# Expert stage of a two-block model: gathered expert rows replaced by both expert tables streamed once

## What is computed

```python
q = (hb @ w_q).reshape(T, 8, 2, 128)
s = einsum('thpc,hpkc->thpk', q, sub_keys)            # 8 heads, 2 halves, 128 keys each
top_s, top_i = top_k(s, 16)
cand_s = top_s[:, :, 0, :, None] + top_s[:, :, 1, None, :]      # 16 x 16 sums
fin_s, fin_pos = top_k(cand_s.reshape(T, 8, 256), 16)
idx = take_along_axis(top_i0 * 128 + top_i1, fin_pos)  # 16 of 16384 experts, per head
gates = softmax(fin_s)
act = gelu(einsum('thkd,td->thk', expert_u[idx], hb))
out = einsum('thk,thkd->td', gates * act, expert_v[idx])
```

## Time and profile before

| what | us |
|---|---|
| three runs | 1610.01, 1617.12, 1620.13 |
| median | 1617.12 |
| span of the profiled execution, first to last instruction | 1608.7 |
| median less that span | 8.4 |

### The profile page before, as it was taken

One profiled execution on the slowest core, in us unless ns is written; L12 is line 12 of the kernel. 1 busy time (PEld: TensorE's weight loads), 2 busy tenths in 40 slices (PEclk: granted clock), 3 DMA queues, 4 the chain that ended last, 5 costly groups with the idle time before them and its releaser, 6 DMA issues.

```text
span 1608.7 us, 22053 instructions
## 1 busy us (share of the span) xinstructions
PE 1490.8 (93%) x7680; PEld 1122.0 (70%) x7682; DVE 944.0 (59%) x2391; ACT 412.9 (26%) x1006; POOL 597.0 (37%) x525
## 2 busy tenths in 40 slices
PE   8999899989899877777799999999999999999997
PEld 7999845554445323223247788999998888899997
DVE  5652587666766776676457734555553145555554
ACT  2110223222222232222115521121123145311112
POOL 4860234334344444443333105555520000455551
PEclk9999999999999999999999999999999999999999
DMA  8464699999999999999994227444424220544431
GB/s 334 157 232 166 256 427 427 426 411 427 427 423 426 425 427 427 427 427 390 426 399 163 76 100 283 166 163 170 139 107 156 105 79 1 213 168 157 157 130 39
DMA packets 63383, 420.63 MB, mean 261 GB/s; under 512 B 7340, under 2 KB 7788, under 8 KB 16812
## 3 DMA queue, kind: packets, MB, share of 16 engines
q0 software_dynamic: 38560, 277.19, 41.5%
q1 hardware_dynamic: 24736, 142.35, 24.8%
HBM read 417.28 MB, written 3.45 MB: 262 GB/s over the span
## 4 chain that ended last, share of the span: by engine, by line
PE 66%; DMA 20%; issue 5%; DVE 4%; POOL 3%; ACT 2%; SPq 0%; POOLq 0%; DVEq 0%
DMA arena<-uv_dram,arena 18%; PE bank L2309 15%; PE wide L2349 9%; PE wide L2110 9%; PE bank L1841 6%; PE bank L1867 4%; PE bank L1960 2%; PE bank L1931 2%; POOL arena L503 2%; PE bank L2476 2%; PE bank L1921 2%; PE bank L2277 2%; PE bank L1818 2%; ACT arena L663 1%; PE bank L2132 1%
## 5 line engine op out<-in xcount | busy, mean ns | idle before, releaser
L2110 PE MATMUL wide<-arena 128*128 128x512 f32 x1024 | 473.0, 609 | 95.7 <-ACT arena L663 95.5
L2110 PEld LDWEIGHTS wide<-arena 128*128 128x128 f32 x1024 | 189.7, 193 | 356.5 <-issue 194.2
L1388 DVE CUSTOM_DVE_ANT_0 arena<-arena,wide 128x1024 f32<-128x1024 f32 x256 | 312.5, 1221 | 191.4 <-DMA arena<-uv_dram,arena 186.5
L503 POOL DMA_INDIRECT arena<-uv_dram,arena x256 | 259.4, 1013 | 405.3 <-PE wide L2110 287.8
L663 ACT ACTIVATE arena<-arena 128x2 f32<-128x2 f32 (+4 forms) x205 | 72.2, 354 | 532.8 <-DVE arena L1388 413.4
L1602 DVE SCALAR_TENSOR_TENSOR arena<-arena,prm 128x255 f32<-128x255 f32 (+1 forms) x152 | 126.0, 849 | 55.6 <-ACT arena L663 55.5
L2349 PE MATMUL wide<-arena,wring 128*128 128x256 f32 x704 | 158.6, 379 | 0.0
L2349 PEld LDWEIGHTS wide<-arena,wring 128*128 128x128 f32 x704 | 130.9, 190 | 16.2
L1636 DVE TENSOR_TENSOR arena<-bank,arena 128x128 f32<-128x128 f32 x266 | 73.9, 290 | 105.2 <-PE bank L2309 101.6
L514 POOL TENSOR_TENSOR arena<-arena 128x512 f32<-128x512 f32 x15 | 20.2, 1349 | 280.8 <-ACT arena L663 280.1
L663 ACT ACTIVATE arena<-bank 128x128 f32<-128x128 f32 (+8 forms) x101 | 40.4, 402 | 303.2 <-PE bank L2309 104.5
(11 more groups left out here) (288 smaller groups left out, 2118.0 us busy)
## 6 DMA issues: line engine op xcount, KB each, us to landing
wring<-ffn_dram SPq DMA_DIRECT2D x43, 1024.0 KB, 5.0
wring<-ffn_dram SPq DMA_DIRECT2D x44, 512.0 KB, 3.5
wring<-win_dram SPq DMA_DIRECT2D x15, 1024.0 KB, 5.3
wring<-wout_dram SPq DMA_DIRECT2D x12, 1024.0 KB, 4.8
wring<-wq_dram SPq DMA_DIRECT2D x5, 1024.0 KB, 7.6
wring<-mix_dram SPq DMA_DIRECT2D x4, 1024.0 KB, 5.3
arena<-uv_dram,arena POOLq DMA_INDIRECT x256, 12.0
wring<-memkv_dram SPq DMA_DIRECT2D x4, 1024.0 KB, 9.4
```

Of the source, the lines that this page charges most:

```text
L503: pool.indirect_dma_start(out=G[:, n % NBUF, :], out_offset=None, in_=a["uv"], in_offset=bass.IndirectOffsetOnAxis(ap=idx[:, u, r:r + 1], ...
L1388: V.tensor_tensor_reduce(out=G[:, n % NBUF, 0:D], in0=G[:, n % NBUF, 0:D], in1=wide[:, 0:2, :].rearrange("p a b -> p (a b)"), scale=1.0, s ...
L2110: ins = MM(wide[:, 2 + h, :], diag[:, n % 4, e, :], G[:, r % NBUF, D + 512 * h:D + 512 * (h + 1)], start=r % (HEADS * TOPK) == 0, stop=r % ...
```

## The change

The gathers are gone. `expert_u` (transposed) and `expert_v` become two more weights of the ring: `xu` and `xv`, 64 loads of 1 MiB each (`XP` = 64). One load holds 256 experts.

- First half, U: for each load p, `unit(p)` on TensorE makes 16 matmuls of 128x128 weights with 256 columns (all tokens): the dot products of 256 experts with 256 tokens, in one bank. ScalarE takes the gelu to `xw[expert in group of 128, group, token]`, 128 x 256 numbers a partition, which stays in SBUF.
- Selection (`pick`) is the same arithmetic as `select`, but for four heads at a time (`HQ`), so 4 calls in place of 16, and the first key, the second key and the gate of each of the 128 picks of a token are kept as numbers (`picked`), turned so that the picks lie on the partitions (`turn_picks`, `keep_picks`). Selection runs on VectorE while TensorE makes the first 32 units (`PLAINX`).
- Spreading the gates: for each token `one_hots` makes two 128x128 matrices on VectorE (one-hot of the first key times the gate; one-hot of the second key), four tokens in a group g, three sets (`HOTS`). Their product on TensorE (`spread_gates`, one 128x128 matmul a token) is the gate of each of the 16,384 experts for that token, in `wide[:, g % 4]`. For groups of experts whose activations are already there, VectorE multiplies them straight into `xw` (`multiply_gates`); for later ones ScalarE copies the gates into `xw` (`keep_gates`), and VectorE multiplies when the unit comes (`multiply_unit`). Eight tokens (`STEP`) are spread in each of the last 32 units.
- Second half, V: for each load p, 16 matmuls of 256 columns sum v times weights over all experts in `wide`, as [channel, token]. No transposes back are needed.
- `wout` is computed for all tokens at once, then normalised, then the queries of eight heads follow one another. The keys of the first memory attention come before the queries, those of the second after V. Some constants grow (`iota` to 128), `wqa`, `wq3`, `wq4` are no longer loaded apart, `memn` of the second layer moves into the ring's spare ends, and `sq_both` and `sq_fin` move in the arena.

```diff
-STREAM = [("win", 16, 2048), ("mix", 4, 2048), ("wout", 4, 2048), ("wq", 5, 2048),
-          ("memkv", 4, 2048), ("glalr", 1, 128),
...
+STREAM = [("win", 16, 2048), ("mix", 4, 2048), ("wout", 4, 2048), ("memkv0", 2, 2048), ("wq", HEADS, 2048),
+          ("xu", XP, 2048), ("xv", XP, 2048), ("memkv1", 2, 2048), ("glalr", 1, 128),
...
-                    pool.indirect_dma_start(out=G[:, n % NBUF, :], out_offset=None, in_=a["uv"],
...
+            def unit(p):
+                g = unit_group(p)
+                pe.wait_ge(freed[TAKER[g - 4]], TAKEN[g - 4])
+                done(project(slot("xu", p), hT, bank[g % 4]))
+            def spread_gates(g):
+                pe.wait_ge(hot_ready, g + 1)
+                if g >= 4:
+                    pe.wait_ge(spread_mul, g - 3)
+                for r in range(4):
+                    ins = MM(wide[:, g % 4, r * 128:(r + 1) * 128], hot[1][g % HOTS][:, r, :], hot[0][g % HOTS][:, r, :], start=True, stop=True)
+                ins.then_inc(spread, 1)
+            queries(0)
+            for h in range(1, HEADS):
+                queries(h)
+                score_rows(h - 1)
+            unit(0)
+            score_rows(HEADS - 1)
+            for p in range(1, PLAINX):
+                if p in TURNS_AT:
+                    turn_picks(TURNS_AT.index(p))
+                unit(p)
+            for p in range(PLAINX, XP):
+                for g in range((p - PLAINX) * STEP // 4, (p - PLAINX + 1) * STEP // 4):
+                    spread_gates(g)
+                unit(p)
+            pe.wait_ge(spread_mul, S // 4)
+            pe.wait_ge(spread_kept, S // 4)
+            for p in range(XP - 2):
+                slot("xv", p)
+                if p >= PLAINX:
+                    pe.wait_ge(freed[DVE_], TAKEN[unit_group(p)])
+                for e in range(2):
+                    for m in range(KT):
+                        ins = values(p, e, m)
+                ins.then_inc(v_used, 1)
...
+            def one_hots(g):
+                if g == 0:
+                    dve.wait_ge(picks_kept, TT)
+                if g >= HOTS:
+                    dve.wait_ge(spread, g - HOTS + 1)
+                rows, cols = hot[0][g % HOTS], hot[1][g % HOTS]
+                V.tensor_tensor(cols, turnedT[:, 1, 4 * g:4 * g + 4].unsqueeze(2).broadcast_to([128, 4, 128]),
+                                C("iota", 128).unsqueeze(1).broadcast_to([128, 4, 128]), ALU.is_equal)
+                for r in range(4):
+                    n = 4 * g + r
+                    ins = V.tensor_scalar(rows[:, r, :], C("iota", 128), turnedT[:, 0, n:n + 1], turnedT[:, 2, n:n + 1],
+                                          ALU.is_equal, ALU.mult)
+                ins.then_inc(hot_ready, 1)
+            def multiply_gates(g):
+                b = g * 4 // STEP
+                i0 = 2 * (PLAINX + b)
+                dve.wait_ge(spread_kept, g + 1)
+                ...
+                o = xw[:, 0:i0, 4 * g:4 * g + 4]
+                V.tensor_tensor(o, wide[:, g % 4, :].rearrange("p (t i) -> p i t", t=4)[:, 0:i0, :], o, ALU.mult).then_inc(spread_mul, 1)
+            def multiply_unit(p):
+                n = STEP * (p - PLAINX + 1)
+                ...
+                o = xw[:, 2 * p:2 * p + 2, 0:n]
+                V.tensor_tensor(o, halves(bank[unit_group(p) % 4])[:, :, 0:n], o, ALU.mult).then_inc(freed[DVE_], 1)
+            pick(0, 0)
+            pick(0, 1)
+            shifted(0)
+            pick(1, 0)
+            gate(0)
+            pick(1, 1)
+            shifted(1)
+            gate(1)
+            for g in range(HOTS):
+                one_hots(g)
+            for p in range(PLAINX, XP):
+                for g in range((p - PLAINX) * STEP // 4, (p - PLAINX + 1) * STEP // 4):
+                    multiply_gates(g)
+                    if g + HOTS < S // 4:
+                        one_hots(g + HOTS)
+                if p > PLAINX:
+                    multiply_unit(p - 1)
+            multiply_unit(XP - 1)
...
+            def keep_gates(g):
+                i0 = 2 * (PLAINX + g * 4 // STEP)
+                act.wait_ge(spread, g + 1)
+                copy(xw[:, i0:NKEYS, 4 * g:4 * g + 4], wide[:, g % 4, :].rearrange("p (t i) -> p i t", t=4)[:, i0:NKEYS, :]).then_inc(spread_kept, 1)
```

More of the change, by code:

```diff
@@ L602, in _ @@
             pool.wait_ge(bias_dram, 48)
+            fold(sq, 8)
+            pool.wait_ge(added, 8)
+            pool.wait_ge(gained0, 8)
+            nc.gpsimd.tensor_tensor(sq_fin, xT[:], xT[:], ALU.mult).then_inc(fin_done, 1)
             for n in range(1, 4):
[L604 to L624, removed]
+                pool.wait_ge(fin_done, n)
+                nc.gpsimd.tensor_tensor(sq_fin[:, 0:2, :], sq_fin[:, 0:2, :], sq_fin[:, 2 * n:2 * n + 2, :], ALU.add).then_inc(fin_done, 1)
             pool.wait_ge(normed, 40)
@@ L796, in keep_head @@
-            def keep_head(stage, h):
-                copy(scores.rearrange("p (t h) n -> p t h n", t=TT)[:, :, h, :], halves(full(stage))).then_inc(freed[ACT_], 1)
-            KEPT_AT = [(5, 7), (6, 5), (7, 3), (7, 7)]
-            scores_half(0, full("scores_a"))
-            for n in range(3):
-                square_t1(n)
-            queries_half(1, 0, full("wqb"))
-            scores_half(1, full("scores_b"))
-            exps(0)
-            square_t1(3)
-            queries_half(2, 0, full("wqc"))
@@ L837, in _, with memory, queries @@
-            act.wait_ge(v_low, 1)
-            copy(peer_o[:, 1, 0:512], wide[:, 2, :]).then_inc(low_out, 1)
+            def memory(l, i):
+                dst = memv[:, l] if i else memk[:, l]
+                copy(dst, halves(full(f"memkv{l}{i}"))).then_inc(freed[ACT_], 1)
+            square(sq, xT, added, [1, 2, 3, 4])
+            memory(0, 0)
+            root("mean_ffn")
+            memory(0, 1)
+            def queries(h):
+                copy(qT[:, 2 * h:2 * h + 2, :], halves(full(f"wq{h}"))).then_inc(freed[ACT_], 1)
@@ L846, in expo @@
+            memory(1, 0)
+            memory(1, 1)
+            act.wait_ge(zeroed, 7)
+            root("mean_mix0", bias=eps2)
             def expo(J):
@@ L1950, in score_rows, with queries @@
+            def queries(h):
+                done(project(slot("wq", h), hT, begin(f"wq{h}"), norms=None if h else 24))
+            def score_rows(h):
+                b = begin(f"scores{h}")
+                pe.wait_ge(freed[ACT_], TAKEN[GROUP0[f"wq{h}"]])
+                for t in range(TT):
                     for j in range(2):
                         hp = 2 * h + j
[L1952 removed]
+                        ins = MM(b[:, (2 * t + j) * 128:(2 * t + j + 1) * 128], qT[:, hp, 128 * t:128 * t + 128],
@@ new lines, in values @@
+            def values(p, e, m, last=False):
+                i = 2 * p + e
+                w = wring[:, (SLOT0["xv"] + p) % RING, :]
+                return MM(wide[:, m // 2, (m % 2) * S:(m % 2 + 1) * S], w[:, e * D + m * 128:e * D + (m + 1) * 128], xw[:, i, :],
+                          start=i == 0 and m % 2 == 0, stop=last and m % 2 == 1)
+            memory(0, 0)
+            mean_folded("mean_ffn", sq, 9)
+            memory(0, 1)
+            pe.wait_ge(ends_in, 32)
+            queries(0)
@@ new lines, in _, with lead @@
+            for n in range(4):
+                for p in (XP - 2, XP - 1):
+                    for e in range(2):
+                        for m in (2 * n, 2 * n + 1):
+                            ins = values(p, e, m, p == XP - 1 and e == 1)
+                ins.then_inc(v_sum, 1)
+            memory(1, 0)
+            memory(1, 1)
+            def lead(stage, b, w, rows, m):
+                for k in range(KT):
+                    if stage == "gla_lr":
+                        pe.wait_ge(gained0, k + 1)
+                    ins = MM(b[0:rows, m * S:(m + 1) * S], w[:, (m * KT + k) * rows:(m * KT + k + 1) * rows], xgm[:, k, :],
```

732 lines of the change are left out of this document (223 added, 509 removed).

## The result

The changed kernel is slower: 1985.48 us median of five runs (1984.76 to 1994.78) against 1611.59 of the kernel before, of five runs too (1610.01 to 1620.13). The ratio is 1.231, 95% interval 1.227 to 1.235. The forecast was 1458, 10% faster. It was wrong in size and in sign.

The account below looks back on a forecast made before the run. It took the kernel before as bound by 268 MB of gathers. With TensorE pacing the new stage, L1841 starts 160.9 us earlier: 1608.7 - 160.9 = 1447.8, plus 8.4 gives 1456, with small bubbles 1458; range 1440 to 1512.

Parts of the forecast that it names:

- A load of U or V is 16 of the first kind: TensorE's price for a load: 16 matmuls of 256 columns, 3.45 us, so 442 us for 128 loads.
- four slots at this same pace: Stretch from 24.5 to 38.3 us, read as TensorE eating four slots without a gap at 345 GB/s.
- arithmetic is only what lies beside them: Gather stage of the kernel before: worth its bytes, 268 MB or 638 us, with arithmetic having no price of its own.
- rival 3: U and V loads: the stream doesn't keep up, loads come singly at 5.3 us, total 1665; chance 0.03.
- things not thought of: Chance of 0.02 left for outcomes outside the forecast and its three rivals.
- forecast 29.2: Selection on VectorE during the plain units: 29.2 us for each call on four heads.
- rival 1: Spreading steps: VectorE bounds them; 1478 if the multiply costs twice as much, 1548 at the worst price; chance 0.17.
- 139 to 141 forecast: Spreading: 32 TensorE steps of 4.35 us, 139.2 in all, about 2 us more where VectorE runs over.
- priced at 4.09: VectorE's average spreading step: one-hots, multiplies and finishing a unit, 4.09 us, against TensorE's 4.35.
- the 8 us: Spreading's multiply: at 1.73 ns an element for hopping reads the sum would be about 8 us longer, 1466.
- The gap before the first spread: After unit 31, TensorE waits for gelu, copied picks and first one-hots; spreading starts at 316.8, second group waits 1.0.
- one load in 3.45 us as forecast: U and V: TensorE takes a load every 3.45 us, 304 GB/s, with the stream taken as hidden.

Follow-up runs that it names:

- half of V: Changed kernel with the second group of experts of each V load left out of the sum for the first 62 loads: 1771.88 us.
- the bf16 version: Changed kernel with U and V cast to bf16, queries, scores and selection staying fp32: 1447.83 us, ratio to the kernel before 0.896.

## Why the prediction was wrong

- **The step that failed** is "A load of U or V is 16 of the first kind", and with it every count of matmuls on the path. It was the price of TensorE's arithmetic, not a wait or an overlap. The pace was right: 3.45 us for 16 and 6.25 us for 56 were read correctly, but of *records*. I multiplied a duration from the profile by a count from the source. A load is 32 records, 6.91 us, and 128 loads are 884 us, not 442. The half of V shows the price of a call directly: 496 calls were worth 214 us, 0.432 each.
- **It stood in my own rows.** `wout` for half of the tokens is 64 calls in the program (four slots, two tiles, eight steps), and the earlier trace rows have x128. The diagonal matmuls are four for a pair of experts and 128 pairs, 512 calls, and the earlier trace rows have x1024. The description of the kernel before even says "4 matmuls for a pair, 1024 in all", which doesn't multiply: 128 x 4 is 512. The stretch from 24.5 to 38.3 us that I took for "four slots at this same pace" has x65 in the earlier trace rows, which is two slots. Comparing one group's count with the loops that make it would have doubled TensorE's terms and turned the forecast round.
- **With the counts doubled the same sum holds.** From 150.1 us: `wout` 27.6, two memory keys and the mean 14.7, eight queries and scores 62.4, U 442, spreads and turnings 58, V 442, two memory keys 13.8, rank and mean 7, then the unchanged 6.4, and 5.5 lost at the first spread (see the last point of this list): 150.1 + 1079.4 = 1229.5. The counterpart of L1841, a call of L1718, starts at 1233.1; up to the end of V (1202.2) the sum is exact to 0.2 us, and the 3.6 missing lie behind it. Start before: 858.2. The difference, 375, is the measured one (374 between the medians). The spans of the two profiled executions differ by 384.3, since the changed kernel's was the longest of its five (1994.78): its work behind that start takes 759.9 us against 750.5, and from 1605 to 1620 us its granted clock is 0.50, the lower level, in the midst of full TensorE work.
- **What bounds the kernel before: right.** Halving the matmuls changed nothing, halving the bytes took 108 us (1504.59 against 1612.76 in the same series). But "arithmetic is only what lies beside them" was loosely argued: that other work hides beside a transfer says nothing of its size when the transfer is gone, and in the run with half of the bytes TensorE was busy for 98% of the stage.
- **The stream (rival 3): rightly put low**, shown by the half of V at 305 GB/s without a gap. The kernel did get slower, but not by this mechanism. The 4.4 us that I took for a transfer from the Trainium skill (DMA: Bandwidth & Descriptors, Anatomy of one DMA) stands there for transfers issued by GpSimd; these loads are issued by SyncE, and their median landing here was 4.8 us, with several in flight. None of my rivals was the one that came: it belongs to the 0.02 for things not thought of. I let TensorE's sum stand without a rival because it was read from clean rows.
- **Selection: right in size, no longer on the path.** In the bf16 version three calls of `pick` start their fourth block (L1271 there) at 264.93, 292.93 and 321.57 us, so 28.0 and 28.6 us apart, forecast 29.2. In the changed kernel TensorE never waits for it. ScalarE takes the second tile's exponentials only after unit 29, so VectorE waits 75 us there, for free.
- **Spreading (rival 1): its mechanism is real, but covered.** With units of 6.91 us, VectorE's step of about 4.5 doesn't show. In the bf16 version, where a unit is short, VectorE is the bound, and 32 steps take 143 us (351.9 to 494.9), 4.5 a step. That this is near the 139 to 141 forecast is luck, since those were TensorE's steps; VectorE's own were priced at 4.09, 131 in all. One price inside the step was off: the one-hot rows, four in 1.11 us and not 0.87 as in the earlier trace rows. The instruction of the earlier trace rows takes one number a partition and does one operation, L1286 takes two numbers and does two; no run separates these. The hops cost nothing (last section), so the 8 us that the Trainium skill's price for them would have added weren't there.
- **The gap before the first spread** was forecast at 2.8 us and a second of 1.0. The rows above show 2.82, and 0.47 at the second. What I had at nothing is the clock behind them: after these idle stretches the granted clock was 0.87 from 479 to 482 us and 0.57 from 482 to 485, between its two levels, and 1.00 again after that. The first step took 14.2 us (476.50 to 490.67) in place of 8.7, so 5.5 were lost, 3.3 of them idle and 2.2 in slower records.

That the bf16 version lands at 1448 where I had forecast 1458 for fp32 is chance: its V is bound by transfers at 2.5 us a load and not by TensorE at 3.45, its plain units by selection, and its calls cost 0.118 us and not 0.216. What shows that the frame of the forecast was sound is the sum above with the doubled counts, and the half of V, where TensorE and the stream ran at one load in 3.45 us as forecast.

## What to carry to other kernels

Before a duration from a profile is multiplied by a count from the source, count the same group in both; in every fp32 group counted here one matmul call is two records. Where a sparse stage becomes dense, price the arithmetic first and the bytes second: here the bytes halved, while 1024 records of TensorE (473.0 us) and 256 dot products of VectorE (312.5 us) became 4096 records of TensorE (884 us). And a stage bound by transfers should be asked what it would be bound by next, since that is what a change that removes the transfers meets.

## What the runs showed of the hardware

- An fp32 matmul of 256 columns costs 0.432 us in two records, a bf16 one 0.118 us in one record. The Trainium skill (FP8 and Floating Point Precision, TensorE Precision Notes) says that a true fp32 product takes four passes through the array. The trace comes near it: by these numbers the fp32 call costs 3.7 times the bf16 one. That each of the two records stands for two passes would fit, but no run here shows it.
- VectorE's multiply read PSUM with a hop of 128 numbers at every element and wrote runs of four at about the plain price: the shortest, 256 elements, took 418 ns and the longest, 504 elements, 683 ns. That is 1.07 ns for each element more, where contiguous reads had 1.03.

```profile
L1300 DVE TENSOR_TENSOR arena<-wide,arena x64: 418/550/683, 482.4 to 753.5; 128x256 f32<-128x256 f32 x2, 128x264 f32<-128x264 f32 x2, 128x272 f32<-128x272 f32 x2, 128x280 f32<-128x280 f32 x2
```

  The Trainium skill (Vector Engine (DVE) Microarchitecture Reference, 5.2 Measured stream behaviour) gives 1.73 ns an element when one source hops at every element. It was measured there on regions of SBUF, and the prediction applied it to a PSUM read. This read doesn't pay it; the measurement decides.
- In the run of the kernel before with half of its matmuls TensorE's granted clock was 0.82 over the stage, a mean between its two levels (436.85 of 650 us busy), against 0.99 with all of them (555.02 busy). The time didn't change, because the engine wasn't the bound:

```profile
196.00:846.00 650.00, 436.85 (x1050) 205.21 (x1049) 441.55 (x1189) 174.35 (x476) 255.17 (x252) 0.82 1.00 421
```
